# A mixture-of-experts decoder step: last three experts fixed, thirteen expert steps instead of fourteen, and state and first input ahead of the order of experts

## The reference, cut to what matters

```python
def _moe(u, w_rg, b_rg, w_re, b_re, w_g, w_u, w_d):
    xf = u.reshape(bsz * t, d)
    p_group = softmax(xf @ w_rg + b_rg); g_sel = argmax(p_group)          # 4 groups
    e_logits = (xf @ w_re + b_re).reshape(-1, 4, 4)                       # 4 experts in each
    top_w, top_i = top_k(softmax(e_logits[g_sel]), 2)
    gates = one_hot(g_sel * 4 + top_i) * (p_g * top_w / sum(top_w))       # (tokens, 16)
    h = silu(einsum('nd,edf->nef', xf, w_g)) * einsum('nd,edf->nef', xf, w_u)   # f = 256
    out = einsum('nef,efd->nd', h * gates[..., None], w_d)
```

## Time and profile before

| what | value |
|---|---|
| median of 3 runs | 541.12 us (540.18 to 541.88) |
| profiled execution, time | 539.75 us |
| its span, first to last instruction | 537.5 us |
| mean granted clock | 0.993 |
| TensorE matmuls busy | 518.3 us, 96% of the span |
| VectorE busy | 259.3 us, 48% |
| ScalarE busy | 151.2 us, 28% |
| GpSimd busy | 155.0 us, 29% |
| moved by DMA | 126.50 MB, mean 235 GB/s |

### The profile page before, as it was taken

How to read it: one execution, slowest core, us unless ns; L and a number is a source line. 1 busy time by engine, 2 the same in 40 slices (tenths; PEclk the granted TensorE clock), 3 DMA queues, 4 the chain that set the end, 5 groups by cost and what they waited for, 6 DMA issues and landing times.

```text
span 537.5 us, 7583 instructions
## 1 busy us (share of the span) xinstructions
PE 518.3 (96%) x2798; PEld 322.0 (60%) x2798; DVE 259.3 (48%) x759; ACT 151.2 (28%) x293; POOL 155.0 (29%) x166
## 2 busy tenths in 40 slices
PE   7999999999999999999999999878999999999994
PEld 6777755554455454557544444557887768668841
DVE  3543465543024223342633276576746766663247
ACT  6332497721122222232222315410100111011132
POOL 3016000116000000000310020336777677777310
PEclk8999999999999999999999999999999999999998
DMA  9999997899900000007931022969998999999574
GB/s 289 357 330 353 340 312 312 306 388 370 333 4 1 0 0 1 1 1 284 382 112 64 39 66 87 382 190 402 364 355 282 365 370 364 365 377 368 124 197 179
DMA packets 47417, 126.50 MB, mean 235 GB/s; under 512 B 6654, under 2 KB 19358, under 8 KB 41234
## 3 DMA queue, kind: packets, MB, share of 16 engines
q1 hardware_dynamic: 30912, 99.36, 50.1%
q0 software_dynamic: 11408, 22.05, 15.0%
q10 hardware_dynamic: 5058, 4.58, 2.5%
HBM read 116.48 MB, written 17.30 MB: 249 GB/s over the span
## 4 chain that ended last, share of the span: by engine, by line
PE 82%; DMA 8%; DVE 5%; issue 2%; ACT 1%; POOL 0%; ACTq 0%; SPq 0%; POOLq 0%; DVEq 0%
PE psum L816 78%; DMA f_dram<-arena,add_tok 5%; PE psum L819 3%; DMA u_dram<-arena 2%; DVE arena L2386 1%; DVE x L2391 1%; DMA arena<-f_dram 1%; DMA hy<-in_c_sample_dram 1%; ACT arena L1502 1%; DVE arena L2187 0%; ACT L1502 0%; POOL f_dram L785 0%; DVE arena L2333 0%; ACT hy L1502 0%; POOL uT L774 0%
## 5 line engine op out<-in xcount | busy, mean ns | idle before, releaser
L816 PE MATMUL psum<-ring,uT 128*128 128x512 f32 (+1 forms) x384 | 126.5, 523 | 0.0
L816 PEld LDWEIGHTS psum<-ring,uT 128*128 128x128 f32 (+1 forms) x384 | 56.7, 173 | 60.0 <-issue 55.7
L1502 ACT ACTIVATE arena<-psum 128x512 f32<-128x512 f32 (+6 forms) x80 | 35.7, 476 | 168.2 <-PE psum L816 150.9
L816 PE MATMUL psum<-uT,ring 128*128 128x288 f32 x256 | 64.9, 411 | 0.1
L816 PEld LDWEIGHTS psum<-arena,ring 128*128 128x128 f32 x512 | 58.5, 192 | 5.9 <-issue 3.9
L816 PE MATMUL psum<-arena,ring 128*128 128x128 f32 x512 | 59.2, 276 | 2.7 <-DVE arena L2187 1.8
L754 POOL DMA_INDIRECT arena<-u_dram,part_tok x52 | 53.4, 1027 | 19.9 <-issue 14.3
L816 PEld LDWEIGHTS psum<-uT,ring 128*128 128x128 f32 x256 | 47.9, 190 | 16.2 <-issue 4.0
L816 PE MATMUL psum<-ring,arena 128*64 128x256 f32 (+2 forms) x192 | 50.6, 490 | 0.0
L785 POOL DMA_INDIRECT f_dram<-arena,add_tok x26 | 41.5, 1598 | 23.1 <-DMA f_dram<-arena,add_tok 13.2
L1502 ACT ACT_TABLE_LOAD x33 | 42.3, 1283 | 3.1 <-issue 2.1
(11 more groups left out here) (260 smaller groups left out, 613.4 us busy)
## 6 DMA issues: line engine op xcount, KB each, us to landing
ring<-in_w_mod_dram SPq DMA_DIRECT2D x24, 1024.0 KB, 11.5
ring<-in_w_exp_down_dram SPq DMA_DIRECT2D x12, 1024.0 KB, 13.4
ring<-in_w_exp_gate_dram SPq DMA_DIRECT2D x11, 1024.0 KB, 9.9
ring<-in_w_exp_up_dram SPq DMA_DIRECT2D x11, 1024.0 KB, 12.5
ring<-in_w_in_dram SPq DMA_DIRECT2D x10, 1024.0 KB, 10.2
ring<-in_w_out_dram SPq DMA_DIRECT2D x4, 1024.0 KB, 6.9
uT<-in_w_exp_gate_dram SPq DMA_DIRECT2D x4, 1024.0 KB, 14.2
f_dram<-in_consts_dram POOLq DMA_DIRECT2D x2, 1536.0 KB, 17.0
```

What stands on the lines that cost most here:

```text
L816: return nc.tensor.matmul(out, lhsT, rhs, start=first, stop=last)
L1502: return nc.scalar.activation(out, src, func, **kw).then_inc(done, 1)
```

## The change

`STEPS` becomes three fixed steps and ten sorted ones with three pairs, at steps 4, 7 and 10; `NST` is 13. The fixed experts are the last three (13, 14, 15), so the sorted ones are experts 0 to 12, and all slices of `order`, ranks, counts and gates follow. `BIG` goes from 9 to 7. On VectorE `new_state(2)` moves ahead of `numbers(1)`, and `take_input(0)` and `new_state(3)` move ahead of `orders()`. On TensorE `add_state(1)` moves ahead of the ranks and changes place with the `keep_running` there, and the `keep_running` ahead of `turn_first` goes. On ScalarE `take_state(1)` moves between the two Exp, and the Silu that loads its table moves behind the store of head 1.

```diff
-STEPS = [()] * FIRST + [(0,), (1,), (9, 10), (2,), (3,), (4,), (11, 12), (5,), (6,), (7,), (8,)]
+STEPS = [()] * FIRST + [(0,), (7, 8), (1,), (2,), (9, 10), (3,), (4,), (11, 12), (5,), (6,)]
...
                 if a < FIRST:
-                    return slice(a, a + 1)
+                    return slice(SORTED + a, SORTED + a + 1)
                 at = STEPS[a][b]
                 if at not in chosen:
-                    chosen[at] = sp.value_load(order[0:1, at:at + 1], min_val=FIRST, max_val=NE - 1)
+                    chosen[at] = sp.value_load(order[0:1, at:at + 1], min_val=0, max_val=SORTED - 1)
...
             pe.wait_ge(s_u2Te, 2 * TILES)
-            keep_running(4, 4)
+            add_state(1)
             pe.wait_ge(s_rsel, 1)
...
             last.then_inc(s_rank, 1)
-            add_state(1)
+            keep_running(4, 4)
...
                     slot_tokens(e)
-                keep_running(4, 3)
                 turn_first()
...
             f(gx[:, :, 0:NG], gx[:, :, 0:NG], ACT.Exp, s_gexp)
+            take_state(1)
             act.wait_ge(s_gin, 2)
             f(gx[:, :, 4:5], gx[:, :, 4:5], ACT.Exp, s_gexp)
-            f(softp[:, 0, 0:1], eps[:, 0:1], ACT.Silu, s_act)
-            take_state(1)
...
                 store_state(1, again)
+                f(softp[:, 0, 0:1], eps[:, 0:1], ACT.Silu, s_act)
...
-                link(v.tensor_tensor(out=masked, in0=rank1[:, :, FIRST:NE],
+                link(v.tensor_tensor(out=masked, in0=rank1[:, :, 0:SORTED],
...
                 hits(1)
                 places()
+                new_state(2)
                 numbers(1)
                 hits(2)
+                take_input(0)
+                new_state(3)
                 orders()
-                take_input(0)
                 numbers(2)
                 gate_weights()
...
                 v.tensor_tensor(out=gates[:], in0=oh[0], in1=oh[1], op=ALU.add).then_inc(s_gw, 1)
-                for h in range(2, NH):
-                    new_state(h)
                 for e in range(NST):
```

More of the change, by code:

```diff
@@ L1848, in take_out @@
                         f(eo[e % 2][:, 0:512], bank[4], ACT.Copy, s_eoa,
-                          scale=gsl[e % 4][:, e:e + 1])
+                          scale=gsl[e % 4][:, SORTED + e:SORTED + e + 1])
                     elif e < NST - 1:
@@ L2331, in hits @@
                     else:
-                        col = rank1[:, t, e:e + 1] if e < FIRST else ranks[e % 2][0][:, t:t + 1]
+                        col = (rank1[:, t, SORTED + e:SORTED + e + 1] if e < FIRST
+                               else ranks[e % 2][0][:, t:t + 1])
                         last = v.tensor_scalar(hit[e % 2][:, t, :], iota16[:], col, None,
@@ L2364, in _ @@
             link(v.scalar_tensor_tensor(
-                out=key, in0=bank[6][:, FIRST:NE], scalar=float(NE),
+                out=key, in0=bank[6][:, 0:SORTED], scalar=float(NE),
                 in1=con[:, C_IOTA:C_IOTA + SORTED], op0=ALU.mult, op1=ALU.subtract))
@@ L2460, in take_out @@
                         dve.wait_ge(s_gs[e % 2], 16 * (e // 2 + 1))
[L2461 removed]
+                        v.tensor_scalar(eo[e % 2][:, 512:1024], bank[5], gsl[e % 4][:, SORTED + e:SORTED + e + 1],
                                         None, ALU.mult).then_inc(s_eod, 1)
@@ L2496, in orders @@
                     link(v.tensor_reduce(out=ordf, in_=grid, axis=AX.X, op=ALU.add))
-                    v.tensor_scalar(order, ordf, float(FIRST - 1), None, ALU.add)\
+                    v.tensor_scalar(order, ordf, -1.0, None, ALU.add)\
                         .then_inc(s_order, 1)
@@ L2507, in pick_gates @@
                                              float(at + 1), None, ALU.is_equal))
-                    link(v.tensor_tensor(out=masked[:, 0], in0=gsl[e % 4][:, FIRST:NE], in1=mine,
+                    link(v.tensor_tensor(out=masked[:, 0], in0=gsl[e % 4][:, 0:SORTED], in1=mine,
                                          op=ALU.mult))
@@ L2556, in _ @@
                         ranks_of(STEPS[NST - 1][0], lastr)
-                        link(v.tensor_tensor(out=masked, in0=gates[:, :, FIRST:NE],
+                        link(v.tensor_tensor(out=masked, in0=gates[:, :, 0:SORTED],
                                              in1=mine.unsqueeze(1)
```

## The result

The changed kernel takes **548.94 us** (median of 4 runs, 547.48 to 549.84) against 540.65 us of the kernel before on the same chip (4 runs, 540.13 to 541.88). The ratio is 1.0147, 95% interval 1.0118 to 1.0177: **slower by 1.5%, 8.3 us**. I forecast slower, at 543.5 and at most 547.5. The sign was right and the size was not: 5.4 us are missing from my sum.

A forecast was written before the change was run, and what follows sets the result against it. TensorE and the DMA loads were both taken as full, with loads limiting 13 steps: stage end 518.0 - 0.2 + 22.1 gave span 539.9, 2.4 above 537.5; put on the 541.12 median, 543.5 us, range 538.0 to 547.5.

The forecast's parts named there:

- TensorE alone at 511.3: End of the expert stage if only TensorE counted: 516.66 + 4.0 + 1.65 - 11.0 = 511.3, or 509.7 without the clock.
- The wait of 1.80 ahead of the up half: TensorE, step 0: the wait for state operations goes, input starts at 359.6, a gain of 2.0 us up to there.
- Order and gates late: VectorE's order ends at 362.7, first late load leaves at 363.5, 3.9 late; gates come at about 366.1, 2.35 late.
- Output of step 1 at 385.2: TensorE's output of step 1 starts 4.0 us later, after some 6 us idle; the clock fall is charged 1.65 us.
- Loads: Late weight loads: 10th lands at 400 to 402, 16th at 424.3, 34th at 492.3 by 3.78 us per load.
- The stage ends at 492.3 + 25.3 = 517.6, and I add 0.4 for a part of a second fall of the clock: Expert stage end: 34th load's landing plus 25.3 us of TensorE work behind it, plus 0.4 for the clock, giving 518.0.
- 6.8 us in hand: Slack in the kernel before: the 34th load lands at 487.7 and is wanted at 494.5, 6.8 us later.
- The end: Last additions, counted from stage end E: the last lands at E - 0.2, then 22.1 us follow; span 539.9.
- Rival D: Pair's additions meet a full load queue and become the tail, landing at E + 4; 547 to 549 us, chance 0.14.
- A: Loads keep up at 3.4 us or less, TensorE sets the end; 535 to 537 us; below 539.5 chance 0.22.
- B: It cancels: loads at 3.70, clock lost once, stage ends about 516; 539.5 to 542.7 us, chance 0.26.
- mechanism C: The forecast itself: the loads are the limit of the 13 steps; 542.7 to 546 us, chance 0.37.

The follow-up runs named there:

- halved loads: Each of the 39 loads behind the order brings half its bytes: in the changed kernel 535.95 us (0.9899), in the kernel before 540.21 us (0.9987).
- the steps alone: The changed kernel with its moved work put back, leaving only the 13 steps: 543.3 us, ratio 1.0057 to the kernel before.
- the two halves of the change: Kernel before with only the moved work, 14 steps: 546.56 us (1.0098); changed kernel with only the 13 steps: 543.3 us (1.0057).
- the late up wait: Up weight waited for only ahead of the up half: kernel before 540.71 us (0.9995), changed kernel 544.85 (1.0084), 13 steps in old work order 538.72 (0.9967).
- the first of the two faster versions: 13 steps with the old order of work, up weight waited for only ahead of the up half: 538.72 us, ratio 0.9967 to the kernel before.

## Why the prediction was right in sign and too small

**Bounds and limits: right.** The reading that both TensorE and the loads are full carried. 14 steps don't notice halved loads; 13 steps wait for whole ones.

**TensorE alone at 511.3: near, by terms that cancel.** 510.94 came with halved loads. In that trace the output of step 1 starts at 384.37, 3.15 us later than before (4.0 forecast), and takes 1.4 more at the lower clock (1.65). From there to the end of the stage TensorE takes 10.2 us less than before, that 1.4 left out; I had 11.0. The sum is 516.66 + 3.15 + 1.4 - 10.2 = 511.0.

**The wait of 1.80 ahead of the up half goes: right**, the input is one group at 361.86. But it starts 2.3 us later than the 359.6 that I took, so TensorE is 0.8 ahead at the input of step 1 (372.85 against 373.67) and not 2.0. And it was worth nothing: what it saved lies ahead of a stall that another engine ends.

**Order and gates late: right in place, too small by 1 to 2 us.** Forecast 363.5 for the first load and 366.1 for the end of the gates, measured 365.36 and 367.39. I had not foreseen that the 13 state matmuls would run at half clock for a good part; the run with fillers ahead of them gave 0.9 back. What makes the clock fall there is left open: the new places of the fillers are not needed for it (it fell in the run with VectorE's moves alone too), and no version with the old order on both engines shows it. In every trace where they ran slow TensorE had stood still for 1.93 to 2.00 us just before them, in every other for at most 1.79; no run tells whether that is the cause. This error was made good by another one, which is luck for the forecast: take_out(0) began 5.8 us after the issue of its gate gather and not 378.59 - 371.76 = 6.8, so at 380.98 where I had 380.95. The shorter time is no accident of one execution. It is 5.7 to 6.3 us in all eight traces of 13 steps with whole loads and 6.8 to 7.1 in the four of 14 steps, and 4.1 and 4.3 with halved loads; I had carried the 6.8 over unchanged.

**Output of step 1 at 385.2 after an idle time, with a fall of the clock: right.** 385.08, of which 2.4 us are the later take_out(0) and 1.5 the longer hits of a pair behind it (4.10 us from take_out(0) to the output against 2.63), and 5.10 - 3.67 = 1.4 us for the clock (I charged 1.65). TensorE's idle time there was 380.2 to 383.7, not from 378.5: I put the end of the input of step 1 too early. The rule that I cited, of "Perfetto Trace Analysis" in the Trainium skill (Matmul Optimizations), that matmuls should come back to back since power follows utilization, agrees with this trace as far as these two places go: the fall was to be paid here and a second time, in full, at step 11. It was not to be paid behind every idle time: after the wait of 2.91 at 481.45 the clock stayed at 1.00.

**Loads: the path right, the 0.1 us in part luck.** By the same two views the 10th landed at 394.50 + 6.7 = 401.2 (forecast 400 to 402), the 16th at 419.81 + 5.3 = 425.1 (424.4), the 34th at 492.2 (492.3): 0.7 too late at the 16th, and then 3.73 us per load where I took 3.78. That the first load left late did not matter. It landed at 371.3 (368.4 forecast), but the next seven came 3.13 us apart (3.53 before), and then TensorE's slots held the loads.

What the sum held and I did not draw out of it is how the moved work reaches the loads. The 16th waits for TensorE to use up its slot, and from its issue on the queue ran the same in seven traces with these 13 steps and whole loads: the 34th lands 72.3 to 72.5 us behind it. With the steps alone the issue is

```profile
414.63 0.33 SPq L563 DMA_DIRECT2D ring<-in_w_exp_gate_dram  x1
```

and the 34th lands at 487.0. In the changed kernel it is 419.81 + 72.4 = 492.2, and with VectorE's moves undone 417.45 + 72.4 = 489.8. So a stall of TensorE at step 1 puts off the loads of step 11 as well. That fits the sum of the two halves of the change, which add up although loads limit 13 steps.

**The step that failed: "The stage ends at 492.3 + 25.3 = 517.6, and I add 0.4 for a part of a second fall of the clock".** Both terms were mis-sized. The 25.3 count from the 34th load, but the code asks for the 35th as well before the first product: 495.50, 3.2 us later. And the second fall costs 2.5 us (6.25 against 3.74), not 0.4, because the wait ahead of it came to be 6.33 us in one piece. 518.0 + 3.2 + 2.1 = 523.3; measured 523.46. In the median these 5.3 are nearly the whole of the missing 5.4 us. The same mistake sits in "6.8 us in hand". Before, the 35th load and the input it is for are

```profile
470.06 0.38 SPq L563 DMA_DIRECT2D ring<-in_w_exp_up_dram  x1
ring<-in_w_exp_up_dram SPq DMA_DIRECT2D x1, 1024.0 KB, 21.4
...
495.02 5.19 PE L816 MATMUL psum<-arena,ring 128*128 128x128 f32 x45
```

that is 470.06 + 21.4 = 491.5 for a start at 495.02: 3.5 us in hand, and 11 were taken. My upper bound of 519.8 left the 35th out too; with 3.2 us more it is 523.0, or 548.5 for the median, beyond the range's end of 547.5. The wait of 6 us that I forecast for TensorE is there: 9.2 measured, 3.2 of them for the 35th.

**The end: right.** The last addition goes out at 518.61 and lands at 523.4 by the chain (518.61 + 4.76), E - 0.1 where I had E - 0.2. The tail behind that landing, 545.6 - 523.4 = 22.2 us, is that of before (22.1). Rival D did not happen: additions in a loaded queue were not what set the end.

**Rivals.** A is refuted by the landing of the 34th at 492.2 and by the waits. Loads closer than 3.5 us, one of my signs of being wrong, did occur, between the 1st and the 8th (3.13), but TensorE waited for none of these, and from the 16th on they came at 3.73. B would have needed loads at 3.70 and one clock loss; there were two. The forecast's mechanism C is what happened, with the 35th load in it.

## What to carry to other kernels

When a step is taken out of an engine that has a supplier at the same rate, measure the slack at the last of the transfers that the next instruction waits for, as the code writes its waits, not at the one that it uses first; moving a wait to where the data is used was worth 3.4 to 4.6 us here, and nothing in the kernel that did not wait for loads. A wait removed ahead of a stall that another engine ends gives nothing, and the work moved to remove it can lengthen the chain of that other engine, here by 5 us. And an idle time on TensorE is to be priced with the clock behind it as a possible second cost: it was 1.4 us at step 1, 2.5 at step 11, and nothing behind the wait at 481.45.

## What the runs showed that I had not expected

An idle time can be filled, and the clock then falls after the next one: with 12 fillers ahead of the 13 state matmuls these ran in 4.01 us, and the input of step 0 behind a later wait of 0.88 us took 9.01 in place of 7.38. Fillers in one gap are no gain by themselves.

The same wait can come with a fall and without. The kernel before with the late up wait stood still for 1.89 us ahead of the up half of step 0 and then took 5.44 us for it; the kernel before, behind 1.80 us, took 3.84, and the first of the two faster versions, behind 1.89 us too, took 3.81. A trace is one execution, and a difference of one or two microseconds between two of them can be such a fall:

```profile
366.15 5.44 PE L816 MATMUL psum<-arena,ring 128*128 128x128 f32 x32 [1.89 <-DVE arena L2189]
```

SyncE's own DMA instructions took long once the queue was deep: 2.77 and 2.82 us for the 34th and 35th loads against 0.37 for the first, and 5.70 for this one:

```profile
474.80 5.70 SPq L563 DMA_DIRECT2D uT<-in_w_exp_up_dram  x1
```

The landings of these loads were some 30 us behind their issues. From the 16th to the 34th the loads landed 3.73 us apart all the same (3.78 before), so these issues cost nothing that a trace here shows.
